# S5's preparation transfers issued by GpSimd, its kernel products a slot later, NSA's gates ahead of compression, MOBA's keys scaled among the values

## The chip, the cores and the metric

One core of a Trainium2 chip runs the whole kernel. The metric is the device time of one execution in microseconds. The engines are TensorE (PE; its weight loads are PEld), VectorE (DVE), ScalarE (ACT), GpSimd (POOL) and SyncE (SP), which only issues transfers. ScalarE and GpSimd issue transfers too; each engine works through one in-order queue of instructions and of waits on semaphores.

## What is computed

Two transformer-like blocks over one sequence of 256 tokens and 1024 features, all in float32:

```python
# first block: RG-LRU layer, SwiGLU, then NSA attention with three branches, SwiGLU, final norm
h = x + rglru_mixer(rmsnorm(x)); h = h + swiglu(rmsnorm(h))
kv = shared_kv(h)                 # keys and values: compressed, selected, window
h = h + nsa_mixer(rmsnorm(h), kv) # softmax(q k) v per branch, times sigmoid gates of rmsnorm(h)
h = h + swiglu(rmsnorm(h)); h = rmsnorm(h)
# second block: half-weight SwiGLU before and after each mixer
h = h + 0.5 * swiglu_2(rms_norm(h)); h = h + s5_mixer(rms_norm(h)); h = h + 0.5 * swiglu_2(rms_norm(h))
h = h + 0.5 * swiglu_2(rms_norm(h)); h = h + moba_mixer(rms_norm(h)); h = h + 0.5 * swiglu_2(rms_norm(h))
```

S5 is a linear recurrence with complex diagonal states. The kernel turns it into products with matrices that depend on the parameters alone: for each of 8 feature tiles (kt) output weights C (cp_s, spilled as s_ca), input weights B (ba_s, spilled as s_ba) and a small kernel K (k_sb, spilled as s_kernel). In MOBA each head's key is divided by its root mean square; in NSA the compressed keys and values come from a two-layer network over 32-token blocks.

## The kernel before

There are ten stages in a row: rglru, ffn, nsa, ffn, ffn, s5, ffn, ffn, moba, ffn. Activations stand feature-major, `h` as 8 tiles of 128 features by 256 tokens. Every large product is made of three passes: the weight is split into a high part (`w_hi`, ScalarE, L880) and a rest (`w_lo`, VectorE, L1325), the activation likewise (`hg_hi`, `hg_lo`), and TensorE adds high x high, high x low and low x high (L2057 to L2059, or L2063 and L2064 where high and low activations go as one wide operand).

**Weights** come in units that SyncE loads into four `raw` buffers; a unit is two halves. A half's split waits until the half four before it is used (`half_used`), so splitting runs four halves ahead. The split of half n+4 stands first in step n of each engine's queue. For a half of 1024 columns TensorE has 24 products of about 0.12 us, or 12 in NSA's compression.

**The FFN stages** have eleven pair slots (0 to 10: gate and up projections) and eight down slots (11 to 18: one output tile of 128 features each, added to `h` by VectorE; `h_written` counts tiles). TensorE asks for tile m's `h_written` before it starts tile m+2. VectorE's row in a down slot is: split a half, two adds into `h`, split a half, `hg_lo` of the tile. GpSimd sums the squares of each written tile: square and add, and before the joint norm (the second FFN's end) a third addition that ScalarE's `scaled_square` two tiles on waits for.

**S5's preparation** is spread over the slots of the first FFN (tiles 0 to 2) and the second (tiles 3 to 7). `C_AT` names the slots in which VectorE makes C (`output_weights`), `K_AT` those in which TensorE makes K's products (`chunk_kernel`, L2197, behind the slot's own products, signalled by `prep_done`) and VectorE keeps it (`keep_kernel`, L1446), `B_AT` those in which VectorE makes B (`input_weights`). The transfers stand in ScalarE's queue (`move_weights`): C's inputs `c_raw` and `b_raw` (`load_c`, which waits for `prep_done` of the tile before), B's inputs `b_rows` and eight `l_rows` (`load_b`), and the three spills. C waits for `c_raw` and `b_raw`, B for its nine, each also for the spill of the tile before.

**NSA** has 52 halves before its attention: 18 of projections (keys and values of three branches; the last two give `v_win`, kept by VectorE at L1752), 16 of compression (18 to 33: keys in bank 0, values in bank 1), 2 of gates (34, 35; `bank[4]`), 16 of q (36 to 51). ScalarE's gelu of the two compressed results stands at j == 33. VectorE scales the gate logits (`gate_f`, L1770) at j == 37; TensorE transposes them there. Between L770 and L774 GpSimd rotates the keys, beside compression.

**MOBA** has 16 halves of q and k, 8 of values (`token_major`, two halves give 256 columns of v for both token halves), then key scales: 16 small products (L2494, recorded as 32) that spread each key's factor over the rows of banks 0 to 3; VectorE multiplies (L1861). Only then come the attention's steps. In `attention` TensorE does scores(0) and scores(1), then for each step n: scores(n+2), transposes of the probabilities, and the products with v; ScalarE exponentiates, VectorE takes maxima and scales.

Of the kernel before, what the change touches and what calls it, by code (L numbers as in the profile page):

```python
# [68 lines left out]
NA_V_BANKS = ((5, 6), (7, 3))  # L69
GLU_BANKS = (0, 1, 2, 3, 5, 6, 7, 4)  # L70
MO_V_BANKS = ((0, 1), (2, 3), (6, 7), (0, 1))
# [21 lines left out]
K_AT = ((9, 12, 16), (2, 6, 10, 13, 16))  # L93
B_AT = ((10, 13, 17), (3, 7, 11, 14, 17))
# [17 lines left out]
def layer_plan():  # L112
# [18 lines left out]
    "nsa": [("q96", 2), ("w8", 1), ("q96", 4), ("w8", 2), ("w8", 4), ("w8", 4), ("gate", 1), ("q96", 8), ("w8", 4)],  # L131
# [32 lines left out]
def two_blocks(nc, ins, out, phases):  # L164
# [4 lines left out]
    with ExitStack() as ctx:  # L169
# [489 lines left out]
        def _(pool):  # L659
# [8 lines left out]
            def sum_squares(norm, ready, scaled=False):  # L668
# [3 lines left out]
                for m in range(KT):  # L672
                    ready(m)
                    if m == 0:
                        pool.tensor_tensor(sumsq[:, :], h[:, m, :], h[:, m, :], ALU.mult).then_inc(sq_step, 1)  # L675
                        steps[0] += 1
                        continue
# [8 lines left out]
                    if scaled:  # L686
                        pool.wait_ge(sqg_made, m + 1)
                        if m >= 2:
                            pool.wait_ge(sumg_made, m - 1)
                        pool.tensor_tensor(sumsq_g[:, :], sumsq_g[:, :], sq_g[:, :], ALU.add).then_inc(sumg_made, 1)  # L690

# [66 lines left out]
            def nsa_phase(ph):  # L758
# [14 lines left out]
                pool.wait_ge(half_used, half0 + 34)  # L773
# [68 lines left out]
            for ph in phases:  # L842
# [13 lines left out]
                if ph["kind"] == "s5":  # L856
                    s5_phase(ph)
                if not ph["last"]:
                    sum_squares(ph["norm"] + 1, lambda m: pool.wait_ge(h_written, h_count(ph["hw"], m)), ph["next"] == "joint")
# [3 lines left out]
        def _(act):  # L863
# [60 lines left out]
            def project(ph, half0, per_tile):  # L924

                for m in range(KT):
# [5 lines left out]
                    if ph["prep"] is not None:  # L932
                        move_weights(ph, PAIRS + m)

            def ffn_phase(ph):
# [17 lines left out]
                if ph["prep"] is not None:  # L953
                    for p in range(PAIRS):
                        pair(p)
                        move_weights(ph, p)
# [8 lines left out]

            def load_c(kt):
                act.wait_ge(prep_done, kt)
                act.dma_start(c_raw[:, :, :], ins["s5_c"][:, kt]).then_inc(c_in, 16)
                act.dma_start(b_raw[:, :, :], ins["s5_b"][:, kt]).then_inc(c_in, 16)

            def load_b(kt):


                if kt:
                    act.wait_ge(ba_made, kt)
                else:
                    act.wait_ge(lp_spilled, 16)
                act.dma_start(b_rows[:, :, :], ins["s5_b_rows"][:, kt]).then_inc(b_in, 16)
                for part in range(2):
                    for row in range(LC):  # L980
                        powers = lp_dram[part, ST * row + 4 * kt:ST * row + 4 * kt + 4, :].rearrange("a n -> (a n)")
                        act.dma_start(l_rows[32 * row:32 * row + 32, part, :], powers[None, :].broadcast_to([32, 4 * P])).then_inc(b_in, 16)

            def move_weights(ph, slot):


                f = ph["prep"]
                tiles = PREP_TILES[f]
                if f == 0 and slot == LAMBDA_AT:
                    s5_lambda()  # L990
                if slot == 0:
                    act.wait_ge(half_used, 2 * ph["u0"])
                    load_c(tiles[0])
                    if f:
                        load_b(tiles[0])
                if f == 0 and slot == ROWS_AT + 1:
                    act.wait_ge(lp_kept, 1)
                    act.dma_start(lp_dram.rearrange("a p n -> p a n"), lp_rows[:, :, :]).then_inc(lp_spilled, 16)
                    load_b(0)
                if slot in K_AT[f]:  # L1000
                    kt = tiles[K_AT[f].index(slot)]
                    act.wait_ge(cp_made, 2 * kt + 2)
                    act.dma_start(ca_dram[kt].rearrange("p (a q n) -> p a q n", a=2, q=4),
                                  cp_s[:, :, :, 1:POW, :].rearrange("p a q t n -> p a q (t n)")).then_inc(ca_spilled, 16)
                    if kt != tiles[-1]:
                        load_c(kt + 1)
                if slot - 1 in K_AT[f]:
                    kt = tiles[K_AT[f].index(slot - 1)]
                    act.wait_ge(k_made, kt + 1)
                    act.dma_start(k_dram[P * kt:P * kt + P], k_sb[:, :]).then_inc(k_spilled, 16)  # L1010
                if slot - 1 in B_AT[f]:
                    kt = tiles[B_AT[f].index(slot - 1)]
                    act.wait_ge(ba_made, kt + 1)
                    act.dma_start(ba_dram[kt], ba_s.rearrange("p a n -> p (a n)")).then_inc(ba_spilled, 16)
                    if kt != tiles[-1]:
                        load_b(kt + 1)
# [116 lines left out]
            def nsa_phase(ph):  # L1133
# [9 lines left out]
                for j in range(52):  # L1143
# [12 lines left out]
                    if j == 33:  # L1156

                        for side in range(2):
                            act.wait_ge(half_used, half0 + 26 + 8 * side)
# [894 lines left out]
        def _(pe):  # L2054
# [400 lines left out]
            def moba_phase(ph):  # L2455
# [20 lines left out]
                for j in range(16, 24):  # L2476
# [6 lines left out]
                    if j == 16:  # L2483
                        mean_of_heads(7)
# [356 lines left out]
```

## Time and profile before

| | us |
|---|---|
| runs of before, median (lowest, highest) | 1853.37 (1850.03, 1853.57) |
| the profiled execution | 1856.77 |
| its span | 1854.8 |
| TensorE busy, its weight loads | 1761.8, 1664.7 |
| VectorE, ScalarE, GpSimd busy | 1312.9, 861.4, 340.0 |
| mean granted clock of TensorE | 0.98 |

The span runs from the first to the last instruction of the one profiled execution; all rows below are on its clock. Busy time of TensorE is modelled from starts, as its products overlap. A row of waits gives the time an engine sat idle before an instruction and what is named as having ended that: where several semaphores are waited for it can be another. "issue" means that the profile shows no releaser.

### The profile page before, as it was taken

The page shows a single profiled execution, that of the slowest core. Times are in us where ns is not written, and L with a number is a line of the kernel's source. Part 1 is how long each engine was busy: PE and PEld are TensorE (multiplying, and loading weights), DVE is VectorE, ACT ScalarE, POOL GpSimd, SP SyncE. Part 2 cuts the span into 40 slices and gives each one's busy share as a digit, 9 for nine tenths or more (in the row PEclk, how much of TensorE's full clock was granted, in tenths as well). Part 3 has the DMA queues.
Part 4 walks back from the last instruction along what each step waited for, and adds up shares of the span by engine and source line. Part 5 has one row for each costly group of instructions (what it writes and reads, how often), then busy time and mean ns, then how long its engine had stood idle before and what let it go on. Part 6 is the DMA issues. An engine that isn't in the chain of part 4 may idle for free. (4 is left out here: it accounts for less than half of the span.)

```text
span 1854.8 us, 32500 instructions
## 1 busy us (share of the span) xinstructions
PE 1761.8 (95%) x13222; PEld 1664.7 (90%) x13222; DVE 1312.9 (71%) x1663; ACT 861.4 (46%) x1133; POOL 340.0 (18%) x305
## 2 busy tenths in 40 slices
PE   7979999998989999889999999999999999889999
PEld 7969998797977999789998888999899989879998
DVE  7897888787565777878866667766666665566663
ACT  5855444254455444434445225444354435355442
POOL 0223001206721200240003103000300036430000
PEclk9989999999989999999999999999999999999999
DMA  7235557446400577655564534456345644425561
GB/s 308 87 114 197 205 202 266 163 165 206 163 13 24 188 235 259 229 178 188 181 224 147 218 112 155 182 183 225 143 175 183 238 146 167 150 92 181 181 224 49
DMA packets 61083, 321.89 MB, mean 174 GB/s; under 512 B 7472, under 2 KB 20336, under 8 KB 30896
## 3 DMA queue, kind: packets, MB, share of 16 engines
q1 hardware_dynamic: 37584, 286.58, 43.2%
q10 hardware_dynamic: 18864, 21.63, 3.9%
q0 software_dynamic: 4528, 12.19, 2.0%
q8 instruction: 75, 1.23, 0.3%
q14 instruction: 32, 0.26, 0.0%
HBM read 309.16 MB, written 10.09 MB: 172 GB/s over the span
## 5 line engine op out<-in xcount | busy, mean ns | idle before, releaser
L1325 DVE TENSOR_TENSOR w_lo<-raw,w_hi 128x1024 fp32r<-128x1024 f32 (+3 forms) x516 | 680.0, 1322 | 326.1 <-ACT w_hi L880 323.8
L880 ACT ACTIVATE w_hi<-raw 128x1024 fp32r<-128x1024 f32 (+3 forms) x516 | 561.5, 1095 | 686.1 <-PE bank L2059 386.0
L2057 PE MATMUL bank<-hg_hi,w_hi 128*128 128x256 f32 (+1 forms) x2672 | 764.9, 286 | 35.2 <-DVE hg_lo L1330 18.6
L2058 PE MATMUL bank<-hg_lo,w_hi 128*128 128x256 f32 (+1 forms) x2672 | 758.5, 284 | 0.0
L2059 PE MATMUL bank<-hg_hi,w_lo 128*128 128x256 f32 (+1 forms) x2672 | 758.2, 284 | 0.0
L2057 PEld LDWEIGHTS bank<-hg_hi,w_hi 128*128 128x128 f32 (+1 forms) x2672 | 512.7, 192 | 41.6 <-DVE w_lo L1325 21.4
L2058 PEld LDWEIGHTS bank<-hg_lo,w_hi 128*128 128x128 f32 (+1 forms) x2672 | 513.0, 192 | 0.3
L2059 PEld LDWEIGHTS bank<-hg_hi,w_lo 128*128 128x128 f32 (+1 forms) x2672 | 512.7, 192 | 0.0
L2063 PE MATMUL bank<-hid,w_hi 128*128 128x512 f32 x1056 | 380.9, 404 | 0.5 <-DVE hid L1492 0.4
L2064 PE MATMUL bank<-hid,w_lo 128*128 128x256 f32 x1056 | 299.4, 284 | 0.0
L2063 PEld LDWEIGHTS bank<-hid,w_hi 128*128 128x128 f32 x1056 | 202.1, 191 | 51.5 <-issue 1.5
L2064 PEld LDWEIGHTS bank<-hid,w_lo 128*128 128x128 f32 x1056 | 203.6, 193 | 0.0
L675 POOL TENSOR_TENSOR sumsq<-h 128x256 f32<-128x256 f32 x9 | 8.7, 969 | 845.7 <-DVE h L1366 845.7
L678 POOL TENSOR_TENSOR square<-h 128x256 f32<-128x256 f32 x63 | 78.5, 1247 | 230.2 <-DVE h L1366 230.2
L681 POOL TENSOR_TENSOR sumsq<-sumsq,square 128x256 f32<-128x256 f32 x63 | 75.9, 1204 | 4.9
L946 ACT ACTIVATE silu_s<-gate_s 128x512 f32<-128x512 f32 x66 | 41.2, 624 | 65.6 <-DVE gate_s L1481 65.6
L950 ACT ACTIVATE hid<-hid_f 128x512 fp32r<-128x512 f32 (+1 forms) x66 | 41.8, 633 | 60.8 <-DVE hid_f L1488 60.8
L1363 DVE SCALAR_TENSOR_TENSOR h<-bank,h 128x256 f32<-128x256 f32 x80 | 33.5, 419 | 49.4 <-PE bank L2064 49.4
L1330 DVE SCALAR_TENSOR_TENSOR hg_lo<-h,vec,hg_hi 128x256 fp32r<-128x256 f32 x72 | 56.6, 794 | 6.2 <-ACT hg_hi L883 6.2
L1485 DVE TENSOR_TENSOR up_s<-bank,rstd 128x512 f32<-128x512 f32 x66 | 45.4, 687 | 19.8 <-PE bank L2059 19.8
L1481 DVE TENSOR_TENSOR gate_s<-bank,rstd 128x512 f32<-128x512 f32 x66 | 45.4, 687 | 16.2 <-PE bank L2059 16.0
L1488 DVE TENSOR_TENSOR hid_f<-up_s,silu_s 128x512 f32<-128x512 f32 x66 | 45.7, 693 | 6.9
(400 smaller groups left out, 2021.6 us busy)
## 6 DMA issues: line engine op xcount, KB each, us to landing
raw<-in_w SPq DMA_DIRECT2D x186, 1024.0 KB, 4.8
raw<-in_w SPq DMA_DIRECT2D x48, 1408.0 KB, 6.1
raw<-in_q SPq DMA_DIRECT2D x14, 768.0 KB, 4.2
raw<-in_w SPq DMA_DIRECT2D x8, 768.0 KB, 4.1
b_rows<-in_s_b_rows ACTq DMA_DIRECT2D x8, 512.0 KB, 5.4
l_rows<-s_powers ACTq DMA_DIRECT2D x64, 64.0 KB, 6.4
s_ca<-cp_s ACTq DMA_DIRECT2D x8, 512.0 KB, 4.2
s_ba<-ba_s ACTq DMA_DIRECT2D x8, 512.0 KB, 3.0
```

Source lines behind the costliest of these rows:

```text
L678: pool.tensor_tensor(square[:, :], h[:, m, :], h[:, m, :], ALU.mult).then_inc(sq_step, 1)
L681: last = pool.tensor_tensor(sumsq[:, :], sumsq[:, :], square[:, :], ALU.add)
L880: act.activation(w_hi[s][:, 0:n], raw[r][:, c * n:(c + 1) * n], ACT.Copy).then_inc(hi_made, 1)
L1325: dve.tensor_tensor(w_lo[s][:, 0:n], raw[r][:, c * n:(c + 1) * n], w_hi[s][:, 0:n].bitcast(F32), ALU.subtract).then_inc(lo_made, 1)
L1330: dve.scalar_tensor_tensor(hg_lo[:, m, :], h[:, m, :], gain(gain_name, m), hg_hi[:, m, :].bitcast(F32), ALU.mult, ALU.subtract).then_inc(h ...
L1481: dve.tensor_tensor(two(gate_s[:, :]), two(gate[:, :]), twice(rstd), ALU.mult).then_inc(gate_scaled, 1)
L1488: dve.tensor_tensor(hid_f[:, :], up_s[:, :], silu_s[:, :], ALU.mult).then_inc(hidf_made, 1)
L2057: pe.matmul(psum, w_hi_ap, x_hi_ap, start=first, stop=False, **kw)
L2058: pe.matmul(psum, w_hi_ap, x_lo_ap, start=False, stop=False, **kw)
L2059: return pe.matmul(psum, w_lo_ap, x_hi_ap, start=False, stop=last, **kw)
L2063: pe.matmul(psum[:, :].rearrange("p (a t) -> p a t", a=2), w_hi_ap, x_pair, start=first, stop=False)
L2064: return pe.matmul(psum[:, 0:T], w_lo_ap, x_pair[:, 0, :], start=False, stop=last)
```

## The change

Four edits:

- `load_c`, `load_b` and `move_weights` move from ScalarE's queue to GpSimd's. In pair slots they stand there one after another, in down slots behind the tile's sum of squares. ScalarE keeps `s5_lambda`.
- `K_AT` and `B_AT` change places: B is made a slot after C, the kernel product a slot after B; VectorE keeps the kernel one slot after the product (and so its spill).
- NSA's gate unit moves ahead of compression (halves 18 and 19; compression is 20 to 35); logits are scaled at j == 19, transposed after half 22, biased at j == 23; gelu stands at j == 35; q takes its banks in the order of `NA_Q_BANKS`.
- MOBA's key scales stand behind the second pair of value halves and go to banks 2, 3, 5, 4; scores of a group wait for that group's keys alone; the last pair of value halves stands behind scores(1), the last two splits of that row and the last v_s behind step 1 of the attention on ScalarE and VectorE.

```diff
+NA_Q_BANKS = (2, 3, 0, 1, 0, 1, 2, 3)
+NA_Q_FREED = {4: 2, 5: 3, 6: 0, 7: 1}
...
-MO_V_BANKS = ((0, 1), (2, 3), (6, 7), (0, 1))
+MO_V_BANKS = ((0, 1), (6, 7), (6, 7), (6, 7))
+MO_KR_BANKS = (2, 3, 5, 4)
...
 C_AT = ((8, 11, 15), (1, 5, 9, 12, 15))
-K_AT = ((9, 12, 16), (2, 6, 10, 13, 16))
-B_AT = ((10, 13, 17), (3, 7, 11, 14, 17))
+K_AT = ((10, 13, 17), (3, 7, 11, 14, 17))
+B_AT = ((9, 12, 16), (2, 6, 10, 13, 16))
...
-    "nsa": [("q96", 2), ("w8", 1), ("q96", 4), ("w8", 2), ("w8", 4), ("w8", 4), ("gate", 1), ("q96", 8), ("w8", 4)],
+    "nsa": [("q96", 2), ("w8", 1), ("q96", 4), ("w8", 2), ("gate", 1), ("w8", 4), ("w8", 4), ("q96", 8), ("w8", 4)],
```

GpSimd's queue takes `load_c`, `load_b` (the same as before, with `pool` for `act`) and `move_weights`, of which this is the core:

```diff
+                if slot in K_AT[f]:
+                    kt = tiles[K_AT[f].index(slot)]
+                    pool.wait_ge(cp_made, 2 * kt + 2)
+                    pool.dma_start(ca_dram[kt].rearrange("p (a q n) -> p a q n", a=2, q=4),
+                                  cp_s[:, :, :, 1:POW, :].rearrange("p a q t n -> p a q (t n)")).then_inc(ca_spilled, 16)
+                    if kt != tiles[-1]:
+                        load_c(kt + 1)
+                if slot - 1 in K_AT[f]:
+                    kt = tiles[K_AT[f].index(slot - 1)]
+                    pool.wait_ge(k_made, kt + 1)
+                    pool.dma_start(k_dram[P * kt:P * kt + P], k_sb[:, :]).then_inc(k_spilled, 16)
+                if slot - 1 in B_AT[f]:
+                    kt = tiles[B_AT[f].index(slot - 1)]
+                    pool.wait_ge(ba_made, kt + 1)
+                    pool.dma_start(ba_dram[kt], ba_s.rearrange("p a n -> p (a n)")).then_inc(ba_spilled, 16)
+                    if kt != tiles[-1]:
+                        load_b(kt + 1)
...
+                if ph["prep"] is not None:
+                    for p in range(PAIRS):
+                        move_weights(ph, p)
...
+                                (lambda m: move_weights(ph, PAIRS + m)) if ph["prep"] is not None else None)
...
-                if slot in K_AT[f]:
-                    keep_kernel(tiles[K_AT[f].index(slot)])
+                if slot - 1 in K_AT[f]:
+                    keep_kernel(tiles[K_AT[f].index(slot - 1)])
```

NSA on TensorE, behind the gate halves, and MOBA on TensorE and on VectorE:

```diff
+                for j in range(20, 28):
+                    hi, lo = weights(half0 + j)
+                    if j == 20:
+                        pe.wait_ge(proj_read, base + 11)
+                        pe.wait_ge(tabs_in, 32)
+                        pe.wait_ge(blklo_made, 1)
...
+                pe.wait_ge(qkf_made, 6)
+                values(0)
+                values(1)
+                pe.wait_ge(qkf_made, 8)
+                key_scales()
+                values(2)
...
                 def step_waits(n):
+                    pe.wait_ge(k_scaled, 2 * att.step(n)[2] + 2)
+                    pe.wait_ge(mask_kept, 1 + ("nsa" in sub_n))
...
+                attention(att, score, pv, step_waits, lambda: values(3), {0: all_keys, 1: all_values})
...
+                def last_values():
+                    keep_values(3)
+                    for j in range(22, 24):
+                        split_lo(half0 + j + SPLIT)
```

## Rows read from the trace of the kernel before

**Rows 1.** The page's part 1: busy time of each engine.
```profile
PE 1761.8 (95%) x13222; PEld 1664.7 (90%) x13222; DVE 1312.9 (71%) x1663; ACT 861.4 (46%) x1133; POOL 340.0 (18%) x305
```
**Rows 2.** TensorE's waits: us in total, times, longest.
```profile
PE bank L2197 <- issue: 14.1, 4, 4.5
PE bank L2381 <- DVE gate_f L1770: 2.3, 1, 2.3
```
**Rows 3.** Windows: us, busy PE, PEld, DVE, ACT, POOL, granted clock, DMA share, GB/s.
```profile
307.00:312.00 5.00, 4.29 (x26) 3.46 (x27) 4.11 (x5) 3.15 (x3) 1.03 (x1) 0.50 0.84 258
...
772.00:778.00 6.00, 5.28 (x29) 4.35 (x30) 5.45 (x7) 1.89 (x3) 2.82 (x3) 0.50 0.79 226
...
802.00:808.00 6.00, 5.76 (x37) 4.80 (x38) 4.97 (x7) 1.44 (x3) 3.30 (x3) 0.72 0.70 165
```
**Rows 4.** Timeline of TensorE, second FFN: start, us, line, tile, idle before.
```profile
772.72 1.08 PE L2197 MATMUL bank<-cp_s,b_raw 128*32 128x128 f32 x16 [4.47 <-issue]
...
802.24 1.08 PE L2197 MATMUL bank<-cp_s,b_raw 128*32 128x128 f32 x16 [3.00 <-issue]
...
823.88 0.39 PE L2057 MATMUL bank<-hg_hi,w_hi 128*128 128x256 f32 x1 [1.64 <-DVE hg_lo L1330]
```
**Rows 5.** Timeline of VectorE, the same stage: C, keeping K, B.
```profile
796.58 2.02 DVE L1420 TENSOR_TENSOR cp_tmp<-c_raw,pc_first 128x1280 f32<-128x1280 f32 x1
...
800.58 1.56 DVE L1424 TENSOR_TENSOR cp_s<-cp_tmp,prep_tmp 128x640 f32<-128x640 f32 x2
...
806.67 0.34 DVE L1446 SCALAR_TENSOR_TENSOR k_sb<-s_par,vec,bank 128x128 f32<-128x128 f32 x1
...
815.60 1.76 DVE L1434 TENSOR_TENSOR ba_s<-l_rows,b_rows 128x1024 f32<-128x1024 f32 x1
...
819.32 0.69 DVE L1438 TENSOR_TENSOR ba_s<-ba_s,prep_tmp 128x512 f32<-128x512 f32 x1
```
**Rows 6.** Landing of b_raw's transfers; GpSimd's timeline, one tile's sums.
```profile
DMA to landing us min/median/max: 5.9/7.6/8.3
...
764.94 1.92 POOL L678 TENSOR_TENSOR square<-h 128x256 f32<-128x256 f32 x1 [6.48 <-DVE h L1366]
...
767.82 1.85 POOL L690 TENSOR_TENSOR sumsq_g<-sumsq_g,sq_g 128x256 f32<-128x256 f32 x1
```
**Rows 7.** Timelines of ScalarE and TensorE around the second FFN's slot 0.
```profile
634.31 2.00 ACT L880 ACTIVATE w_hi<-raw 128x1024 fp32r<-128x1024 f32 x2 [6.37 <-issue]
...
636.77 0.36 PE L2057 MATMUL bank<-hg_hi,w_hi 128*128 128x256 f32 x1 [1.52 <-DVE w_lo L1325]
```
**Rows 8.** NSA: timelines of VectorE and TensorE, and a window (as rows 3).
```profile
419.52 0.87 DVE L1752 TENSOR_SCALAR v_win<-bank,rstd_tok 128x256 f32<-128x256 f32 x2
...
420.50 0.44 PE L2057 MATMUL bank<-w_hi,blk_k_hi 96*60 96x256 f32 x1 [3.30 <-DVE w_lo L1325]
...
420.00:435.00 15.00, 14.29 (x98) 14.06 (x99) 9.59 (x8) 7.73 (x8) 10.89 (x10) 0.78 0.58 196
...
427.03 26.72 DVE L1325 TENSOR_TENSOR w_lo<-raw,w_hi 128x1024 fp32r<-128x1024 f32 x15 [1.34 <-ACT w_hi L880]
...
450.80 0.29 PE L2057 MATMUL bank<-hq,w_hi 128*48 128x256 f32 x1
...
453.69 0.33 PE L2057 MATMUL bank<-hq,w_hi 128*96 128x256 f32 x1
```
**Rows 9.** MOBA: timelines of VectorE, TensorE and ScalarE.
```profile
1605.69 0.87 DVE L1854 TENSOR_SCALAR v_s<-bank,rstd_tok 128x256 f32<-128x256 f32 x2
...
1611.44 0.87 DVE L1854 TENSOR_SCALAR v_s<-bank,rstd_tok 128x256 f32<-128x256 f32 x2
...
1612.45 3.81 PE L2494 MATMUL bank<-mo_tab,qk_rstd 128*128 128x128 f32 x32 [3.34 <-DVE v_s L1854]
...
1618.46 0.69 DVE L1663 TENSOR_REDUCE sb_small<-bank 128x4 f32<-128x512 f32 x1 [1.48 <-PE bank L2274]
...
1630.29 0.58 ACT L1100 ACTIVATE mo_prob<-bank,sb_small,qk_rstd 128x256 f32<-128x256 f32 x1
```

More of the change, by code:

```diff
@@ L666, in _, with load_c, load_b @@
             pool.memset(eps_2, EPS * EPS).then_inc(pool_const, 1)
-            def sum_squares(norm, ready, scaled=False):
+            def load_c(kt):
+                pool.wait_ge(prep_done, kt)
+                pool.dma_start(c_raw[:, :, :], ins["s5_c"][:, kt]).then_inc(c_in, 16)
+                pool.dma_start(b_raw[:, :, :], ins["s5_b"][:, kt]).then_inc(c_in, 16)
+            def load_b(kt):
+                if kt:
+                    pool.wait_ge(ba_made, kt)
+                else:
+                    pool.wait_ge(lp_spilled, 16)
+                pool.dma_start(b_rows[:, :, :], ins["s5_b_rows"][:, kt]).then_inc(b_in, 16)
+                for part in range(2):
+                    for row in range(LC):
+                        powers = lp_dram[part, ST * row + 4 * kt:ST * row + 4 * kt + 4, :].rearrange("a n -> (a n)")
+                        pool.dma_start(l_rows[32 * row:32 * row + 32, part, :], powers[None, :].broadcast_to([32, 4 * P])).then_inc(b_in, 16)
@@ new lines, in move_weights @@
+            def move_weights(ph, slot):
+                f = ph["prep"]
+                tiles = PREP_TILES[f]
+                if slot == 0:
+                    pool.wait_ge(half_used, 2 * ph["u0"])
+                    load_c(tiles[0])
+                    if f:
+                        load_b(tiles[0])
+                if f == 0 and slot == ROWS_AT + 1:
+                    pool.wait_ge(lp_kept, 1)
+                    pool.dma_start(lp_dram.rearrange("a p n -> p a n"), lp_rows[:, :, :]).then_inc(lp_spilled, 16)
+                    load_b(0)
+                if slot in K_AT[f]:
[15 more added lines that the diff above has]
+                        load_b(kt + 1)
@@ L670, in sum_squares @@
+            def sum_squares(norm, ready, scaled=False, after=None):
                 if norm >= 1:
@@ L676, in sum_squares @@
                         steps[0] += 1
+                        if after:
+                            after(m)
                         continue
@@ L690, in sum_squares @@
                         pool.tensor_tensor(sumsq_g[:, :], sumsq_g[:, :], sq_g[:, :], ALU.add).then_inc(sumg_made, 1)
+                    if after and m >= 1:
+                        after(m)
             def rglru_phase(ph):
@@ L951, in pair @@
                                    hid_f[:, :], ACT.Copy).then_inc(hidhi_made, 1)
[L953 removed]
+                if ph["prep"] == 0:
                     for p in range(PAIRS):
                         pair(p)
[L956 removed]
+                        if p == LAMBDA_AT:
+                            s5_lambda()
                 else:
@@ L964, in ffn_phase @@
                 project(ph, half0 + 4 * PAIRS, 2)
[L966 to L999, printed above, removed]
-                if slot in K_AT[f]:
[L1001 to L1016, printed above, removed]
@@ L1187, in moba_phase @@
                 att = Attention("moba")
-                for j in range(24):
+                for j in range(22):
                     split_hi(half0 + j + SPLIT)
@@ L1834, in moba_phase, with keep_values @@
                 half0 = 2 * ph["u0"]
-                for j in range(24):
+                def keep_values(u):
+                    dve.wait_ge(half_used, half0 + 18 + 2 * u)
+                    for b in range(2):
+                        dve.tensor_scalar(v_s[:, b, T * u:T * u + T], bank[MO_V_BANKS[u][b]][:, 0:T], rstd_tok[:, b:b + 1],
+                                          None, ALU.mult).then_inc(proj_read, 1)
+                for j in range(22):
                     split_lo(half0 + j + SPLIT)
```

146 lines of the change are left out of this document (69 added, 77 removed).

## The prediction

> **What bounds the kernel now.** I read the page's busy times first, then TensorE's waits, then the timeline around each long wait, then the windows with the granted clock. TensorE is busy for 95% of the span, VectorE for 71%, ScalarE 46%, GpSimd 18% [rows 1]. So the time is TensorE's products plus its holes, and only a hole that goes, or a stretch at the lower clock that goes, shortens the run. The diff can touch four kinds of holes: the waits before S5's kernel products, 14.1 us together, and before NSA's gate transposes, 2.3 us [rows 2]; the wait before NSA's compression, and those around MOBA's key scales (both below).
>
> Two things lie around S5's waits. **The clock**: in the stretch from 307 us the granted clock is 0.50, from 772 us 0.50, from 802 us 0.72 [rows 3], at 772 and 802 right behind a wait of 3 us or more [rows 4]. That is the lower of its two levels (1.2 of 2.4 GHz) for some of the stretch. Loss is (1 - clock) x stretch less what was idle anyway: 2.15, 2.65 and 1.7 us; the fourth place, the second of the first FFN, is taken as 2.4. Together 9 us. **Who was late**: VectorE's cp_s ends at 800.58 + 1.56 = 802.1, the product starts at 802.24 [rows 4, 5]. C stands in down slot 12 or 15 (11 or 15 in the first FFN) and the product one slot later, and such a slot is 7.7 us of TensorE: between 772.72 and 802.24 lie three tiles, 29.5 - 3.0 wait - 1.1 product - 2.3 clock = 23.1 [rows 4].
>
> **S5's products a slot later.** C takes VectorE 5.6 us (796.6 to 802.1), the tile's own five operations 4.6 (802.1 to 806.7), B 4.4 (815.6 to 820.0) [rows 5]. With the product two slots behind C, cp_s is some 7 us early and the wait is gone, if nothing takes its place. Late next is VectorE itself: C and B now stand in adjacent slots, 10.2 + 9.0 = 19.2 us of work in 15.4 of TensorE's, where a light slot stood between them. That lag of 3.8 us is below one slot, and h_written of tile m is asked for at tile m+2, w_lo four halves ahead, so TensorE doesn't see it. In the first FFN c_raw and b_raw are issued at the last pair slot, 11 us ahead of C, and land in 7.6 [rows 6]. Its two waits (14.1 less the second FFN's 4.47 + 3.00) and their clock (2.15 + 2.4) go: 6.6 + 4.6 = **11.2 us**.
>
> **The second FFN** is less kind. load_c(kt+1) sits behind prep_done(kt+1) in GpSimd's queue, and from slot 11 on behind a tile's sum of squares too: GpSimd starts on it when h is written, needs 3.5 to 4.7 us (764.94 to 769.67) [rows 6], then issues s_ca and load_c. I step it from the end of tile 0, 752.8 (772.72 - 4.47 - 2 x 7.7). VectorE, B in pair slot 10 behind it, writes h(0) at 758; GpSimd gets to load_c(6) at 760, it lands at 768; VectorE is ready for C(6) at 765 and waits 3 us. C to 773.2, B to 782.4, h(3) at 784.9; GpSimd 3.5, s_ca 0.5, two issues 1.1, landing 7 to 7.6: load_c(7) is there at about 797. VectorE, ready at 792, waits 4 to 5 us, and from there its queue is the chain: C to 802, tile 5 to 807, B to 811, tiles 6 and 7 and hg_lo(7) at about 819. TensorE pays 0.5 to 1 us before product 7, 1.5 before tile 7, 3 to 4 at the next stage's start. That stage now gets its last hg_lo at 823.88 [rows 4]. So of 7.5 + 1.6 us of waits and 4.3 of clock, 823.9 - 819.2 = **4.7 us** is gained. With transfers that land at once it would be about 9.5; each microsecond of landing costs up to two (two C slots wait in series).
>
> **The issues' move itself.** At the second FFN's first slot ScalarE issues eleven transfers (load_c, load_b), its next w_hi waits 6.37 us for that (0.58 each), and TensorE 1.52 us for w_lo [rows 7]. There is a second such place, shorter. Both go: **2 us**. GpSimd has nothing else in the pair slots, so its issues cost nothing there; in the down slots nine of them, some 5 us, stand between two sums of squares that are 8 us apart and take 4.7. The next sum may start 2 us late, which only ScalarE's scaled_square of two tiles on could see. The last k spill leaves behind GpSimd's last sum and lands some 5 us after the last h; VectorE waits for it at NSA's start, where it has room: 0, at worst 1.5. In the last tile's slot the queue delays mean_square by one issue at most, and TensorE asks for that two halves into the next stage. How fast GpSimd's queue lands under this load no row shows. The same transfer on ScalarE's took 5.9 to 8.3, 7.6 in the middle [rows 6]; I take 7.6, with ends 5.9 and 12 (half as much again, as its descriptors come from an engine that shares work with VectorE).
>
> A page speaks against the move. SBUF — State Buffer in the Trainium skill, section "SBUF: two separate sides", says that descriptors of a GpSimd-issued transfer can't be written while VectorE holds the port pair they share, and gives about 3.1 us in place of 0.62. By it each landing would be up to 2.5 us later and the sum 5 us smaller; no run shown here has such a transfer beside these VectorE operations.
>
> **NSA.** TensorE stops at 417.2 and starts the first compression half at 420.50; what it waits for is v_win (419.52 + 0.87 = 420.4), not the w_lo that the profile names. The clock in that stretch is 0.78, of 15 us [rows 8]: some 2.7 us lost beside the hole. The two gate halves take 450.80 to 453.69, 2.9 us [rows 8]. Put at 417.2 they fill the hole, and compression starts at 420.4 at full clock. TensorE alone would gain 2.9 + 2.7 = 5.6. But from 427 on compression goes at VectorE's pace: 15 w_lo in 26.72 us, back to back [rows 8], about 2.1 us for a full one, while GpSimd's rotations share its port, against 1.4 us of TensorE. VectorE gets into this row earlier, since the gate halves free their slots at 418.6 and 420. Stepped, it reaches the last one about 447.5 with 0.7 for the gates' own reads, and q starts at 449.0 in place of 453.69: 4.6. The wait before the transposes, 2.3, goes, since gate_f is made before they are asked for. The gelu stays hidden: banks 2 and 3 come first in q. Together **6.9 us**, ends 3 and 9.
>
> **MOBA.** TensorE ends the values at 1609.1, waits 3.34 us for the last v_s (w_hi, w_lo, then v_s in VectorE's queue, 1611.44 + 0.87), and does 3.81 us of key scales [rows 9]. A pair of value halves is 1611.44 - 1605.69 = 5.75. After: key scales at 1597.7 to 1601.5 without a wait, two value halves to 1607.3, scores(0) at once. VectorE starts the first maximum at 1610.4 in place of 1618.46. The last value halves lie where TensorE waits for exponentials. But two w_hi (2.1), a v_s (0.9) and two w_lo (2.5) now stand in ScalarE's and VectorE's attention queues: the third maximum is at 1622.3, and from there it goes as before but for a wait less: the last exponentials begin at 1627.4 in place of 1630.29 [rows 9]. **2.9 us**, ends 1 and 4.
>
> **The sum**: 11.2 + 4.7 + 2 + 6.9 + 2.9 = 27.7 us. The profiled execution took 1856.8 us (span 1854.8), the median of the runs is 1853.4; 1856.8 - 27.7 = 1829.1 and 1853.4 - 27.7 = 1825.7. The runs are what is asked: **1826 us**.
>
> **Rivals.** (a) *VectorE holds GpSimd's transfers up.* A transfer that waits for one or two of its operations (2.02 the longest) lands 2 to 4 us later; in the second FFN's two C slots that is 4 to 8, with one more fall of the clock (2.5): 1832 to 1836. For: VectorE is never free there. Against: nothing in NSA, where GpSimd's transfers run beside VectorE, shows TensorE waiting for one. Chance 0.20. That page's rule is this rival. (b) *VectorE doesn't wait for c_raw in the second FFN* (faster landing, shorter sums): 5 us more, 1821, down to 1815 with NSA's upper end. 0.14. (c) *The clock falls anyway*, at the small holes that remain: the waits go but not the losses, 27.7 - 9 - 2.7 = 16: 1837. Against: it stayed full past MOBA's 3.34 us (3.81 us for 32 products, 0.12 each, [rows 9]). 0.08. (d) *Slower*: the queue starves at the C slots. If a landing takes 7.6 + x, the cost is 2x in the second FFN and x - 3.2 in the first; 3x - 3.2 meets 27.7 at x = 10, a landing of 18 us. At 20 us: 1859. It needs over twice the longest landing of that tile. 0.03. (e) *The holes come back elsewhere*, as waits for VectorE: 1852. 0.02. The forecast has the rest, 0.53, with its own range 1819 to 1832.
>
> **Range and chances.** 8 in 10 takes (b), the forecast, and most of (a) and (c): 1814 to 1841. A measurement of this kernel tells about 0.2% (3.7 us) from no change: faster 0.95 (forecast, a, b, c), same 0.02 (e), slower 0.03 (d).
>
> **What would show it.** Right: no wait before the kernel products in the first FFN and a clock near 1.00 there; VectorE waiting for c_raw's or b_raw's transfer at slots 12 and 15 of the second; gate products at 417, no half clock at 420, q at about 449; scores(0) of MOBA 10 us ahead of its old place, the projection only 3. Wrong: the clock still falls at these places, b_raw lands in over 10 us, or w_lo in compression takes more than 2.2 us.

## The result and the profile after

The changed kernel takes **1826.51 us** (1824.48 to 1828.20) where the kernel before took 1852.16 beside it: a ratio of 0.9866, interval 0.9849 to 0.9882. In a later session it had 0.9837 (0.9818 to 0.9857), so two sessions can differ by 0.3%, and small differences are read below from stages of the profiles. The forecast was 1826, within 1814 to 1841. The number held; the reason given for its largest term did not.

TensorE's timeline of the changed kernel, first instructions of stages and what it waited for (start, us, line, tile, idle before):

```profile
354.90 0.36 PE L2080 MATMUL bank<-hg_hi,w_hi 128*96 128x256 f32 x1 [0.27 <-DVE hg_lo L1342]
...
408.02 0.30 PE L2080 MATMUL bank<-w_hi,blk_k_hi 96*60 96x256 f32 x1 [0.50 <-issue]
...
436.86 0.36 PE L2080 MATMUL bank<-hq,w_hi 128*96 128x256 f32 x1 [0.33 <-DVE w_lo L1337]
...
591.40 0.39 PE L2080 MATMUL bank<-hg_hi,w_hi 128*128 128x256 f32 x1 [0.71 <-DVE hg_lo L1342]
...
775.37 0.65 PE L2220 MATMUL bank<-cp_s,b_raw 128*32 128x128 f32 x16 [1.63 <-DVE k_sb L1458]
777.60 0.50 PE L2086 MATMUL bank<-hid,w_hi 128*128 128x512 f32 x1 [1.59 <-DVE h L1378]
...
793.17 0.58 PE L2080 MATMUL bank<-hg_hi,w_hi 128*128 128x256 f32 x1 [3.95 <-DVE hg_lo L1342]
...
1594.67 1.38 PE L2307 MATMUL bank<-mo_tab,mo_prob 128*128 128x128 f32 x8 [3.09 <-DVE mo_prob L1695]
1597.23 3.78 PE L2534 MATMUL bank<-mo_prob_t,v_s 128*128 128x128 f32 x16 [1.18 <-ACT mo_prob_t L1119]
...
1633.92 0.39 PE L2080 MATMUL bank<-hg_hi,w_hi 128*128 128x256 f32 x1 [0.70 <-DVE hg_lo L1342]
```

The waits of 3 us and more before the kernel products [rows 4] are gone; one of 1.63 is left, the last. In NSA compression starts without the 3.30 us of [rows 8], and q comes 82.0 us behind the stage's start in place of 86.3. New are the waits at 775 to 793 us and the one at 1594.67. Windows (us, busy PE, PEld, DVE, ACT, POOL, granted clock, DMA share, GB/s), and behind them the page's busy times:

```profile
300.00:312.00 12.00, 12.00 (x71) 10.53 (x71) 11.93 (x14) 4.66 (x4) 3.31 (x3) 1.00 0.82 272
793.00:797.00 4.00, 3.83 (x19) 3.84 (x20) 1.59 (x3) 1.06 (x1) 1.93 (x3) 0.57 0.99 283
1594.67:1600.00 5.33, 4.15 (x21) 3.75 (x22) 2.91 (x7) 4.25 (x14) 0.00 (x0) 0.56 0.40 168
```
```profile
PE 1749.9 (96%) x13222; PEld 1656.1 (91%) x13222; DVE 1315.3 (72%) x1663; ACT 863.6 (47%) x1133; POOL 399.8 (22%) x418
```

The clock is full where [rows 3] had 0.50, but the mean of a window is between its two levels, 1.2 and 2.4 GHz, behind the two long waits that are new (0.57 and 0.56). TensorE is busy for 11.9 us less with the same instructions, GpSimd for 59.8 more, its issues. The two executions by stages, each from first product to first product:

| stage | before | after | gained | predicted |
|---|---|---|---|---|
| first FFN | 204.3 | 191.2 | 13.1 | 11.2 |
| NSA | 246.7 | 236.5 | 10.2 | 6.9 |
| second FFN | 209.8 | 201.8 | 8.1 | 4.7 + 2 |
| up to the first product behind the joint norm | 15.1 | 16.6 | -1.5 | 0 |
| from there to the stage behind MOBA | 825.6 | 824.2 | 1.4 | 2.9 |

With 0.6 us lost ahead of the first FFN this is 30.6 us, the spans' difference (1854.8 to 1824.2). The profiled execution of before lay 4.6 us above its median, that of after on its own; the medians' difference is 25.7. Some of this is in the first FFN: the same instructions took 204.3 us here, but 202.1 and 201.1 in the profiles of MOBA's and NSA's part alone (below), which leave that stage as it was. So its gain is 9.9 to 13.1 us, by the execution that one compares with. The second FFN took 209.6 to 211.9 in these three.

One thing that the four edits don't name changes too: with the transfers gone, ScalarE's pair slots 1 to 8 of the second FFN run as a loop, where they were written out. The instructions in them are the same.

### The profile page after: what moved, and what is told of

The parts are those of the page before. It is cut to its first block, busy times and chain, and to the rows that moved or that the text cites. A ratio compares the mean times of both kernels' runs of the same rounds, so it can differ in the third digit from the quotient of the medians.

```text
span 1824.2 us, 32533 instructions
## 1 busy us (share of the span) xinstructions
PE 1749.9 (96%) x13222; PEld 1656.1 (91%) x13222; DVE 1315.3 (72%) x1663; ACT 863.6 (47%) x1133; POOL 399.8 (22%) x418
## 4 chain that ended last, share of the span: by engine, by line
PE 81%; DVE 13%; ACT 3%; issue 2%; DMA 1%; POOL 1%; ACTq 0%; DVEq 0%; POOLq 0%
PE bank L2080 17%; PE bank L2081 17%; PE bank L2082 17%; PE bank L2086 14%; PE bank L2087 7%; DVE w_lo L1337 5%; ACT w_hi L941 1%; PE bank L2297 1%; PE bank L2452 1%; DVE hg_lo L1342 1%; DMA b_raw<-in_s_b 1%; PE bank L2307 1%; PE bank L2279 1%; PE bank L2566 1%; PE bank L2280 1%
## 5 line engine op out<-in xcount | busy, mean ns | idle before, releaser
L1337 DVE TENSOR_TENSOR w_lo<-raw,w_hi 128x1024 fp32r<-128x1024 f32 (+2 forms) x516 | 682.5, 1328 | 284.2 <-ACT w_hi L941 282.3
L941 ACT ACTIVATE w_hi<-raw 128x1024 fp32r<-128x1024 f32 (+2 forms) x516 | 563.8, 1096 | 655.3 <-PE bank L2082 407.3
L2086 PE MATMUL bank<-hid,w_hi 128*128 128x512 f32 x1056 | 373.1, 397 | 1.6 <-DVE h L1378 1.6
L1009 ACT ACTIVATE hid<-hid_f 128x512 f32 (+1 forms) x66 | 41.8, 634 | 52.6 <-DVE hid_f L1500 52.6
L1497 DVE TENSOR_TENSOR up_s<-bank,rstd 128x512 f32<-128x512 f32 x66 | 45.4, 688 | 22.6 <-PE bank L2082 22.6
L1493 DVE TENSOR_TENSOR gate_s<-bank,rstd 128x512 f32<-128x512 f32 x66 | 45.4, 688 | 18.4 <-PE bank L2082 18.2
```

What stands on the lines that cost most here:

```text
L941: act.activation(w_hi[s][:, 0:n], raw[r][:, c * n:(c + 1) * n], ACT.Copy).then_inc(hi_made, 1)
L1337: dve.tensor_tensor(w_lo[s][:, 0:n], raw[r][:, c * n:(c + 1) * n], w_hi[s][:, 0:n].bitcast(F32), ALU.subtract).then_inc(lo_made, 1)
L1493: dve.tensor_tensor(two(gate_s[:, :]), two(gate[:, :]), twice(rstd), ALU.mult).then_inc(gate_scaled, 1)
L2086: pe.matmul(psum[:, :].rearrange("p (a t) -> p a t", a=2), w_hi_ap, x_pair, start=first, stop=False)
```

## The experiments

### Which part carries the gain: four parts, each alone on the kernel before

The slots alone, with ScalarE still issuing:

```diff
-K_AT = ((9, 12, 16), (2, 6, 10, 13, 16))
-B_AT = ((10, 13, 17), (3, 7, 11, 14, 17))
+K_AT = ((10, 13, 17), (3, 7, 11, 14, 17))
+B_AT = ((9, 12, 16), (2, 6, 10, 13, 16))
...
-                if slot in K_AT[f]:
-                    keep_kernel(tiles[K_AT[f].index(slot)])
+                if slot - 1 in K_AT[f]:
+                    keep_kernel(tiles[K_AT[f].index(slot - 1)])
```

> The kernel before with the slots alone: the product stands two slots behind C, B between them, VectorE keeps K a slot later; the transfers stay in ScalarE's queue. My theory: the waits in front of the kernel products and the falls of the clock behind them carry the gain of this edit, whoever issues. Then the first FFN gives about 12 us and the second 5 to 8, and the time is 1833 to 1838. Rival: the slots need GpSimd's queue, since ScalarE's now waits for VectorE's k_sb within the same slot (two slots behind C) and its next w_hi comes late; then at most half of it comes, 1841 to 1846, and VectorE waits for w_hi in the down slots.

Measured: **1876.95 us**, ratio 1.0124 (1.0105 to 1.0143), 24.8 us slower. Both times fail; the rival's mechanism is there, but is not all. The waits before the products did go, and others took their place and more. TensorE's longest group in the second FFN is now (us in total, times, longest):

```profile
PE bank L2063 <- DVE h L1366: 10.2, 4, 4.6
```

ScalarE's timeline in the same stage shows how:

```profile
805.33 0.52 ACTq L1003 DMA_DIRECT2D s_ca<-cp_s  x1
...
805.89 0.68 ACTq L968 DMA_DIRECT2D c_raw<-in_s_c  x1
806.60 1.12 ACTq L969 DMA_DIRECT2D b_raw<-in_s_b  x1
807.76 0.46 ACTq L1014 DMA_DIRECT2D s_ba<-ba_s  x1
808.26 0.67 ACTq L978 DMA_DIRECT2D b_rows<-in_s_b_rows  x1
808.96 4.85 ACTq L982 DMA_DIRECT2D l_rows<-s_powers  x8
813.91 2.64 ACT L880 ACTIVATE w_hi<-raw 128x1408 fp32r<-128x1408 f32 x2 [7.68 <-PE bank L2064]
...
826.23 2.65 ACT L880 ACTIVATE w_hi<-raw 128x1408 fp32r<-128x1408 f32 x2 [7.55 <-DVE k_sb L1446]
```

The new slots put all thirteen issues of a tile into one slot, 8.5 us ahead of the next w_hi, and a slot later ScalarE waits for VectorE's k_sb, another 7.6. VectorE then waits for w_hi, TensorE for VectorE: 32.3 us in the two FFN stages, 20.3 before.

The move of the transfers alone, with the old slots (the diff shown ahead, without its constants and keep_kernel):

> The kernel before with the transfers moved to GpSimd's queue alone; products, B and K stay in their old slots. My theory: the move by itself is worth the 1.5 us wait at the second FFN's first slot and a shorter one, 2 us: 1850; the waits in front of the kernel products stay (14 us together), and load_c(7) is issued at about the same time as before, as the old slots leave it 12 us. Rival (VectorE holds GpSimd's transfers up, landing 2 us and more later): the waits grow and the time is 1853 to 1858, with b_raw landing in over 9 us.

Measured: **1838.19 us**, ratio 0.9920 (0.9900 to 0.9939), 13.9 us faster, seven times what I had given it. Theory and rival both fail. The waits before the four late products are not as they were either; TensorE's timeline:

```profile
306.22 0.65 PE L2202 MATMUL bank<-cp_s,b_raw 128*32 128x128 f32 x16 [1.16 <-issue]
...
339.31 0.65 PE L2202 MATMUL bank<-cp_s,b_raw 128*32 128x128 f32 x16 [1.17 <-issue]
...
757.06 0.64 PE L2202 MATMUL bank<-cp_s,b_raw 128*32 128x128 f32 x16 [2.31 <-issue]
785.76 1.08 PE L2202 MATMUL bank<-cp_s,b_raw 128*32 128x128 f32 x16 [3.02 <-issue]
```

They were 3.23, 3.44, 4.47 and 3.00; 7.7 us are left of 14.1, and the clock in the first FFN is full. VectorE's waits for w_hi in the second FFN, of before, of the slots alone and of the queue alone (line waited for: us in total, times, longest):

```profile
DVE w_lo L1325 <- ACT w_hi L880: 38.7, 22, 6.4
```
```profile
DVE w_lo L1325 <- ACT w_hi L880: 54.3, 22, 9.3
```
```profile
DVE w_lo L1330 <- ACT w_hi L938: 25.0, 26, 3.0
```

In both FFN stages together: before 69.1, the slots alone 92.6, the queue alone 45.4, the changed kernel 35.7. These agree with one chain, which the run with B's inputs alone (below) tests: ScalarE's issues delay w_hi, w_hi delays VectorE, VectorE makes C late, and TensorE waits for C.

NSA's part alone (gates ahead of compression, order of q's banks; MOBA's banks as before):

> The kernel before with NSA's part alone: gates ahead of compression, the order of q's banks. The stage gained 10.2 us in the changed kernel, of which 7.1 stand at the gate transposes and 3 come later, in an attention whose waits are the same but whose granted clock is higher (0.84 against 0.74 just behind the transposes). Theory: the 3 us belong to this edit, as the attention is entered without a wait of 2.3 us: 1842. Rival: they hang on where the stretch falls in time, not on the edit: 1845 to 1846, the clock again 0.74 there.

Measured: **1844.52 us**, ratio 0.9956 (0.9940 to 0.9972), 7.6 us less. The median lies between the theory and the rival; the stage is 236.6 us long, 10.0 less than in the kernel before. Over all kernels of this study NSA took 242.0 to 249.0 us in the six with the old order and 232.0 to 237.2 in the eight with the new one. The means differ by 10.6, of which 8.3 lie ahead of the attention (7.1 between the kernel before and the changed one). The rest is in the attention, whose waits are nearly the same. It took 105.1 to 106.3 us in five of the six and 100.5 in the sixth, and 100.1 to 105.3 with the new order. In its first 22 us the granted clock is 0.74 or 0.75 in those five and 0.84 in the sixth, with the new order 0.79 to 0.92. So the edit goes with more clock, but one execution with the old order had as much: that the clock's share is the edit's doing is not shown, and what the clock depends on there is left open.

MOBA's part alone:

> The kernel before with MOBA's part alone. In the changed kernel the stage gained 1.4 us in place of 2.9: the exponentials are as early as predicted, but TensorE waits 3.1 us for the second step's probabilities, and behind that the clock falls to 0.56. Theory: both belong to this edit: 1851 (1.4 us less). Rival: the fall of the clock is due to where the stretch falls in time; then this kernel keeps the full clock and gains 3: 1849.

Measured: **1851.57 us**, ratio 0.9995 (0.9980 to 1.0010): no gain that can be told from none. TensorE waits 3.10 us for the probabilities and the window behind that has half the clock, as the theory has it:

```profile
1622.00:1628.00 6.00, 4.83 (x22) 4.42 (x23) 2.96 (x8) 4.08 (x13) 0.00 (x0) 0.50 0.30 126
```

### What of ScalarE's queue it was

Only B's inputs (b_rows, eight l_rows a tile) are issued by GpSimd, on the kernel before:

```diff
+            def load_b(kt):
...
+                pool.dma_start(b_rows[:, :, :], ins["s5_b_rows"][:, kt]).then_inc(b_in, 16)
```

> The kernel before with only B's inputs (b_rows and eight l_rows a tile) issued by GpSimd; C's inputs and the spills stay with ScalarE, all slots are the old ones. The whole queue's move gave 13.9 us with the old slots. Theory: it is the nine issues in a row, 5 us of ScalarE's queue ahead of its next w_hi, that make VectorE late, and so the products; then this part has most of it, 8 to 12 us: 1840 to 1844, VectorE's waits for w_hi fall from 69 us in the two FFN stages to about 50, and the waits in front of the kernel products shrink to 1 to 3 us each. Rival: the gain lies in C's inputs and the spills (their issue takes ScalarE about 1.1 us for b_raw alone), or in the landing of C's inputs: 1848 to 1852.

Measured: **1839.43 us**, ratio 0.9930 (0.9913 to 0.9947), 13.7 us less than before beside it: all of what the whole move gave. VectorE's waits for w_hi fall to 46.7 us, the waits before the products to 1.3, 1.8, 2.7 and 3.0. It is the 72 issues of B's inputs; with the old slots, C's inputs and the spills could have stayed. With the new slots that was not run. Here ScalarE's second FFN is still written out, and the stage takes 202.9 us as with the whole queue's move, where it is a loop: the loop carries nothing.

The slots alone once more, but K's spill a slot later in ScalarE's queue:

```diff
-                if slot - 1 in K_AT[f]:
+                late = 1 if slot == PAIRS + KT - 1 else 2
+                if slot - late in K_AT[f]:
```

> The kernel before with the new slots, the transfers still in ScalarE's queue, but each spill of K one slot later there, so that ScalarE doesn't wait for VectorE's k_sb of the same slot. With the slots alone the time was 1877, 24.8 us over the kernel before; VectorE waited 92.6 us for w_hi in the two FFN stages in place of 69.1. Theory: ScalarE's wait for k_sb (7.6 us in front of its next w_hi, at each of the later tiles) is the main part of that; the rest is that the product's, B's and C's issues now fall into one slot (8.6 us in a row at 805 us). Then this kernel takes 1855 to 1865. Rival: the row of issues is nearly all of it, 1870 to 1877.

Measured: **1867.84 us**, ratio 1.0084 (1.0059 to 1.0108), between the two ranges: 15.2 us over before in place of 24.8. NSA happened to be 7.0 us shorter than with the slots alone, by the clock; the two FFN stages, which are what was edited, are 9.8 shorter (204.2 + 219.1 against 209.0 + 224.1). So ScalarE's wait for k_sb is near half of the 19 us that these stages had lost. The other half is put down to the row of issues, by what is left; no run takes it away by itself.

The changed kernel with the old slots put back, and the changed kernel again beside it:

> The changed kernel with the old slots put back (the product one slot behind C, B behind it, K kept in the product's slot); GpSimd's queue, NSA's and MOBA's parts stay. By the profiles the two FFN stages and the joint norm behind them gave 19.6 us in the changed kernel and 16.7 with the queue's move alone. Theory: the slots are worth 2 to 4 us once GpSimd issues: 1828.5 to 1831 in a session where the changed kernel takes 1826.5, with waits of 1.2, 1.2, 2.3 and 3 us ahead of the kernel products again. Rival: the slots are worth nothing or less there, as VectorE's waits for b_raw and TensorE's last holes come with them: 1824 to 1827.

> The changed kernel once more, beside the others on the same chip: 1826.5, a ratio of 0.986 to the kernel before.

Measured: 1830.57 us, ratio 0.9869 (0.9845 to 0.9894), against **1822.73**, 0.9837 (0.9818 to 0.9857). By stages the slots bring 3.6 us in the first FFN and 1.0 in the second, and cost 1.5 at the joint norm: 3.1, as the theory has it. The first FFN took 191.2 us in each of the six kernels with the new slots and GpSimd's queue, and 194.5 to 194.9 in the three with the old slots whose B inputs GpSimd issues, so these 3.6 are well clear of what varies there. The rest of the medians' 7.8 is mostly NSA (236.4 against 232.0), which this edit doesn't touch. The intervals overlap, so the times alone don't show it.

### The second FFN's end: is it VectorE's wait for b_raw?

In the changed kernel GpSimd's timeline is this:

```profile
756.81 1.92 POOL L733 TENSOR_TENSOR square<-h 128x256 f32<-128x256 f32 x1 [5.01 <-DVE h L1378]
758.82 0.81 POOL L736 TENSOR_TENSOR sumsq<-sumsq,square 128x256 f32<-128x256 f32 x1
759.70 2.00 POOL L745 TENSOR_TENSOR sumsq_g<-sumsq_g,sq_g 128x256 f32<-128x256 f32 x1
761.65 0.89 POOL L706 DMA_DIRECT2D s_ca<-cp_s  x1
762.48 0.62 POOL L673 DMA_DIRECT2D c_raw<-in_s_c  x1
763.03 0.60 POOL L674 DMA_DIRECT2D b_raw<-in_s_b  x1
```

VectorE's next C starts at 769.86, behind a wait of 6.04 for this b_raw. The edit puts load_c and then cp_s's spill ahead of the down slot's sum (and load_c ahead of the spill in the pair slots); of it, the place in the loop over the tiles:

```diff
                 for m in range(KT):
+                    if first:
+                        first(m)
                     ready(m)
```

> The changed kernel with load_c and the spill of cp_s ahead of the tile's sum of squares in GpSimd's down slots. Theory of the prediction: VectorE's waits for b_raw in the second FFN (1.6 and 6.0 us) come from the sum that stands ahead of the issue, and TensorE's last holes there (1.6, 1.6, 0.3, 0.3 and 4.0 us) and the fall of the clock behind them (1.5 us) come from those waits. Then both waits go and 6 to 8 us are gained: 1818 to 1820.5. Rival: VectorE is full there anyway, or GpSimd's later sums hold TensorE up: 1824 to 1828.

Measured: **1817.81 us**, ratio 0.9809 (0.9786 to 0.9833). GpSimd issues c_raw at 752.29 and b_raw at 752.87, VectorE waits for neither, and TensorE has one hole left:

```profile
788.30 0.39 PE L2089 MATMUL bank<-hg_hi,w_hi 128*128 128x256 f32 x1 [1.79 <-DVE hg_lo L1351]
```

The stage and the stretch behind it take 195.2 and 15.1 us in place of 201.8 and 16.6: 8.1 us. The theory holds, the loss behind the joint norm included.

Another way to the same, C every three slots:

```diff
-C_AT = ((8, 11, 15), (1, 5, 9, 12, 15))
-K_AT = ((10, 13, 17), (3, 7, 11, 14, 17))
-B_AT = ((9, 12, 16), (2, 6, 10, 13, 16))
+C_AT = ((8, 11, 15), (1, 4, 7, 10, 13))
+K_AT = ((10, 13, 17), (3, 6, 9, 12, 15))
+B_AT = ((9, 12, 16), (2, 5, 8, 11, 14))
```

> The changed kernel with C in slots 1, 4, 7, 10, 13 of the second FFN, B a slot and the product two slots behind it: a tile every three slots, the last C two slots earlier. Same theory: with one C less in the down slots, and one more slot of VectorE's time behind the last, TensorE's last holes go: 5 to 8 us, 1818.5 to 1821.5, if the pair slots carry it (VectorE is busy for 84% there). Rival: in the pair slots C waits for its inputs, which are issued just a slot ahead, and VectorE's w_lo come late: 1826 to 1832.

Measured: **1816.82 us**, ratio 0.9805 (0.9780 to 0.9829). VectorE waits 3.2 us for b_raw once, the holes at the end are 0.61 and 1.10, the two stretches take 195.3 and 15.1: 7.9 us. The pair slots carry it.

### MOBA: who holds the probabilities up

The last two w_hi go behind step 3 of the attention, their w_lo behind step 4; the last v_s stays behind step 1:

```diff
-                attention(att, {1: last_weights})
+                attention(att, {3: last_weights})
...
-                attention(Attention("moba"), {1: last_values})
+                attention(Attention("moba"), {1: lambda: keep_values(3), 4: last_rests})
```

> The changed kernel with MOBA's last two w_hi behind step 3 of the attention and their w_lo behind step 4, in place of step 1 for both. Theory: the wait of 3.1 us for the second step's probabilities is VectorE's, held by the two w_lo (2.4 us, and 2.3 of waiting for w_hi), and the fall of the clock to 0.56 behind it is that wait's doing: both go, 2.5 to 4 us: 1822.5 to 1824. Rival: the wait only moves to the next exponentials, or to w_lo at the projection's start: 1826 to 1827, and the clock falls just the same.

Measured: **1820.00 us**, ratio 0.9823 (0.9802 to 0.9844); by the stage 5.9 us (818.3 against 824.2), 2 more than expected. VectorE's timeline of this kernel, then of the changed kernel:

```profile
1587.30 0.69 DVE L1675 TENSOR_REDUCE sb_small<-bank 128x4 f32<-128x512 f32 x1 [0.24 <-PE bank L2296]
...
1588.31 1.23 DVE L1695 TENSOR_TENSOR mo_prob<-mo_prob,sb_small 128x1024 f32<-128x1024 f32 x1
```
```profile
1590.11 2.36 DVE L1337 TENSOR_TENSOR w_lo<-raw,w_hi 128x1024 fp32r<-128x1024 f32 x2 [2.25 <-ACT w_hi L941]
1592.38 0.68 DVE L1675 TENSOR_REDUCE sb_small<-bank 128x4 f32<-128x512 f32 x1
...
1593.39 1.22 DVE L1695 TENSOR_TENSOR mo_prob<-mo_prob,sb_small 128x1024 f32<-128x1024 f32 x1
```

The probabilities come 5 us earlier, there is no wait of 3.1, and the clock stays at 1.00 from 1588 to 1608. In the changed kernel the sixteen v products behind the hole took 3.78 us, here 2.05. With the wait the fall is gone as well, here and in the kernel with all three edits below, while all six kernels that have the wait have a fall behind it. So the fall was the wait's doing; of the stage's 5.9 us it had some 2.8.

### All three together

> The changed kernel with the three edits that each gained: C's inputs and cp_s's spill issued ahead of the sum of squares (8.7 us less in its session), C every three slots in the second FFN (9.7), MOBA's last splits behind steps 3 and 4 (6.5). The first two take away the same holes at the second FFN's end: the first leaves a wait of 1.8 us at the next stage's start, the second 0.6 and 1.1 us. Theory: together 10 to 11 us, and MOBA's 6 by itself: 1809 to 1811. Rival: they overlap wholly, the better one alone counts: 1811 to 1813; or MOBA's gain hangs on where it falls: 1815.

Measured: **1812.95 us** (1809.22 to 1814.98), ratio 0.9787 (0.9768 to 0.9807), the lowest median of the study; its interval overlaps those of the three edits alone, so the times don't show that all three are better than the best of them. The changed kernel beside it has 0.9837. By stages, against the changed kernel's first profile, the second FFN and the stretch behind it give 8.8 us, MOBA 6.7. The first two edits overlap almost wholly (8.8 against 8.1 and 7.9 alone), as the rival had it; MOBA's adds up. But these are 15.5 us, and the ratios give 9.3. The profiled execution of the changed kernel beside it and that of the three edits differ by 12.8 (spans 1820.1 and 1807.3): NSA was 2.8 us shorter in the former (232.0 against 234.8), and the latter lay 3.7 us below its own median.

## Why the prediction was right, and where it was not

The parts add up: the queue alone 13.9 us, NSA alone 7.6, MOBA alone 0.5 and the slots 3.1 by stages are 25.1 of the 25.7. That the forecast lay within 1 us of the median is in part luck. The two FFNs with the joint norm gave 19.7 us where 17.9 were forecast, NSA 10.2 for 6.9, MOBA 1.4 for 2.9; with 0.6 lost ahead of them the profiles' total is 30.6 for 27.7, and the medians' difference was 25.7 in one session and 30.2 in the other.

**S5's products a slot later, 11.2 us: the amount came (13.1), the cause was wrong.** I asked who was late, found VectorE's C, and stopped there. The step that failed is "the wait is gone, if nothing takes its place": with the slots alone the waits are gone and others do take their place. VectorE had waited 69 us for ScalarE's w_hi in the two stages, of which 45 are left with the queue's move alone and 36 in the changed kernel, and I had not read VectorE's own waits. The slots alone cost 24.8 us; the queue alone shortens the first FFN by 9.8, the slots add 3.6 there once the queue has moved. The 1.9 us above the forecast are clock: my 2.15 came from a window that ended at 312 us, and 2.4 was a guess, while the clock was low for longer at both places:

```profile
307.00:314.00 7.00, 6.29 (x33) 5.17 (x34) 5.54 (x7) 3.15 (x3) 2.72 (x2) 0.51 0.86 257
344.00:352.00 8.00, 6.21 (x33) 5.12 (x34) 6.49 (x9) 0.51 (x1) 2.65 (x2) 0.57 0.36 99
```

That is 3.4 us at each of the two by (1 - clock) x stretch, before what was idle anyway is taken off. The other two executions of this stage, at 202.1 and 201.1 us, lost less.

**The issues' move, 2 us: 13.9 measured.** Mis-sized. I priced the one wait that TensorE shows for it, 1.52 us [rows 7], and not the 6.37 of ScalarE beside it as something that repeats with every tile. Nine issues of about half a microsecond, for each of eight tiles, stand ahead of w_hi in an engine that I had at 46% [rows 1] and so took for idle. The sum came out all the same because the slots' gain and the queue's are gains on the same holes: I gave nearly all to the one, and by the runs most belongs to the other.

**The second FFN, 4.7 us: the waits right, the credit wrong.** VectorE waits 1.6 and 6.0 us for b_raw where I had 3 and 4 to 5; TensorE pays 1.63, 1.59 and 3.95 where I had 0.5 to 1, 1.5 and 3 to 4. The stage gave 8.1, but the queue's move alone gives 6.9 there; once it has moved, the slots bring 1.0 in the stage and lose 1.5 at the joint norm. So the 4.7 us that I gave to the slots are not theirs, as in the first FFN. What I cost at nothing was the clock behind the last of these waits: 0.57 at 793 us, 1.5 us up to the joint norm. Issued ahead of the sums, all of it goes.

**NSA, 6.9 us: 10.2.** 4.3 to q's start (4.6 taken), 7.1 with the transposes' wait. The other 3.1 are clock in the attention, which I had not looked at, since nothing there was edited. By the spread between executions above, they may be chance.

**MOBA, 2.9 us: 1.4 by the stage; alone, its time can't be told from no gain.** The last exponentials begin at 1597.54; before's 1630.29 less the 29.2 us by which everything ahead of MOBA had moved is 1601.1, so they are 3.5 us early, more than the 2.9 taken. But I followed the exponentials alone. TensorE asks for the second step's probabilities before them, and they stood behind the two w_lo: 3.1 us of waiting, and a fall of the clock that I had argued away with one case, the 3.34 us after which it had stayed full [rows 9].

**The rivals.** (a) didn't come: b_raw lands 3.3 to 7.0 us after its issue, 5.5 in the middle, against 7.6 on ScalarE's queue [rows 6]. The one that was waited for longest, issued at 763.03, was under way while VectorE sat idle for 6.04 us, so VectorE didn't hold it up. The forecast had taken the rule of the Trainium skill (SBUF — State Buffer, "SBUF: two separate sides") for this rival, and that was a misreading: the page ties the hold-up to VectorE operations in a two-port mode, and says that in its own probe `tensor_tensor` did not stall the transfer. VectorE's preparation work is nearly all TENSOR_TENSOR [rows 5], and with that the trace agrees: b_raw's issues took 0.54 to 0.61 us. l_rows do land later in the changed kernel (8.1 us in the middle, ScalarE's 6.4), but with the old slots GpSimd's took 4.9. The longer row of issues in one slot may be why; that is not shown, and nothing waits for them. (b) is what the two later versions reach: with b_raw in time the kernel is at 1817 to 1818. (c) came in two places, for 1.5 us and about 3. (d) and (e) didn't come for the whole change, but the slots alone are a case of (d)'s size, by a mechanism that I hadn't named: too many issues of one slot in one queue.

## What to carry to other kernels

Before an edit is priced, follow the late engine's own waits one step further: an engine that is 46% busy can hold the others up through where its transfers stand in its queue. A transfer's issue cost the issuing engine about half a microsecond here, so put rows of small ones on the queue that nobody waits for, and ahead of long work there. When two edits take away the same hole, their prices don't add, and only each alone tells which one works: here one of them alone is a loss of 25 us.

## What the runs showed of the hardware that was not expected

- An issue takes ScalarE 0.44 to 1.95 us for l_rows (0.48 in the middle) and 1.06 for b_raw; GpSimd 0.50 to 0.59 and 0.55. A spill of B is the other way: 0.33 on ScalarE, 0.60 on GpSimd. The 112 issues that moved took 65.7 us on ScalarE and 64.1 on GpSimd. So GpSimd was the steadier place, even beside VectorE's work, but not a cheaper one; what counts is what stands behind the issue:

```profile
L982 ACTq DMA_DIRECT2D l_rows<-s_powers x64: 442/478/1952, 269.1 to 799.3; - x64
```
```profile
L687 POOL DMA_DIRECT2D l_rows<-s_powers x64: 496/505/591, 263.8 to 768.1; - x64
```

(before and after; ns, least/middle/most.) The Trainium skill (Perfetto Trace Analysis, "DMA Optimizations") says that balancing transfers across the engines that can issue them may help where making their descriptors is the bottleneck. Here it gave 13.7 us, by taking the issues out of the way of ScalarE's next w_hi.
- The same wait isn't always followed by the same clock. MOBA's 3.1 us stand in six kernels; in the 6 us behind them the clock is 0.50 to 0.58 in five and 0.72 in one. The 3.34 us in front of the old key scales stand in six others: the scales took 3.81 us in four and 5.44 in two. The one case that I argued from, [rows 9], was one of the four. So a fall behind such a hole is priced with a chance, and it can cost as much as the hole.
- NSA's length differs by up to 5 us between kernels that are the same there, mostly by the clock: of the 4.5 us between the changed kernel's two executions (236.5 and 232.0), 3.1 lie in the attention, at a clock of 0.95 and 0.98. That is as much as two of the edits were worth, and a reason to compare stages and not only times.
